# A decoder block with gathered experts: 32 more tokens leave the dense u pass, low parts of u move to GpSimd beside the gates, and v weights are made in pairs

## The chip, the cores and the metric
The kernel runs on one core of one Trainium2 chip. The metric is device time in microseconds, the median of several runs. Engines: TensorE (PE) multiplies matrices, VectorE (DVE), ScalarE (ACT) and GpSimd (POOL) work on elements, SyncE (SP) issues transfers. SBUF is on-chip memory of 128 partitions, PSUM takes TensorE's results.

## The reference
512 tokens of width 1024 pass one block: a norm with modulation, three kinds of attention, an output projection, then a feed-forward part with 16,384 experts, and a last norm. Nearly all the time behind the attention is the expert part:

```python
q = einsum('td,de->te', xc, wq)                  # 8 heads x 2 sides x 128
s = einsum('thpd,hpnd->thpn', q, sub_keys)       # 128 keys a side
sv, si = top_k(s, 16)                            # best keys of each side
cand = sv[:, :, 0, :, None] + sv[:, :, 1, None, :]
top, pos = top_k(cand, 16)                       # 16 experts a head, 128 a token
g = softmax(top)
a = gelu(einsum('thkd,td->thk', u[eidx], x))     # u, v: 16384 x 1024, float32
return einsum('thk,thkd->td', g * a, v[eidx])
```

## The kernel before, in words
The expert part is done in two ways. Tile 0 (128 tokens) is done by gathering: for each of its 128 expert slots GpSimd gathers 128 rows of u and of v, VectorE takes a dot with u and adds v times its weight. The other 384 tokens (DT) are done densely: the experts stand in 128 chunks of 128, and for each chunk TensorE makes all dots of u with all tokens (`a_chunk`, 24 matmuls), the result goes through gelu, is multiplied by a gate that is zero where a token did not choose the expert, and multiplies v (`v_chunk`, 18 matmuls of 512 columns). Float32 is kept by splitting each operand into a rounded high part and a low rest: three products in place of one. ScalarE rounds (`u_hi`, `v_hi`), VectorE or GpSimd subtracts (`u_lo`, `v_lo`).

The order is written out by hand. First the q and score matmuls; VectorE picks the top 16 of each (`best16`, two heads at a time, after every fourth q pass) and decodes numbers (`decode`). Meanwhile TensorE starts on the u chunks. 64 chunks (and chunk 64) come "early": chunks 0 to 23 alone, then for each of three tiles four gate blocks of 32 tokens, with two u chunks beside each block, and gaps of u chunks alone between them (4, 8 and 4 chunks), in which VectorE decodes the next tile. A block has eight groups of four tokens. For a group VectorE makes `hot_i` (four operations: key numbers compared with a token's column, times the gate, L2057) and `hot_j` (L2059); TensorE multiplies them into a table of gates, ScalarE copies it to `g_out` and stores the whole block to DRAM at its end (2 MB). hot_i and hot_j have two buffers. VectorE makes the low part of every u chunk from 17 on (L2002, `split_u`), GpSimd of those before.

Then comes the mixed loop: for each chunk m, v of chunk m, then u of chunk m + 65, as long as there are u chunks (63 times); VectorE multiplies gelu by gate, rounds it and subtracts (`weigh`), makes v's and u's low parts, and works 12 to 14 gathered rows of tile 0 in eight chunks. The last 60 chunks have v alone, less four at the end in another order. Gates come back from DRAM four chunks at a time into g_in (512-byte pieces). The mixed loop can start when the last block's gates are stored and the first group is loaded.

## Time and profile before
| | |
|---|---|
| median of 3 runs | 1567.66 us (1567.62 to 1569.81) |
| span of the profiled execution | 1565.4 us |
| TensorE busy | 1527.4 us (98%) |
| VectorE busy | 1337.7 us (85%) |
| ScalarE busy | 660.1 us (42%) |
| GpSimd busy | 487.5 us (31%) |
| DMA | 398.77 MB, mean 255 GB/s |

The span is from the first to the last instruction of the profiled execution; the profile gives no other time for that execution, and the median of the runs lies 2.3 us above it. Matmuls are pipelined and their ends are modelled, so a busy TensorE can still be slower than it could be; starts say more than durations.

### The profile page before, as it was taken

How to read it: one execution, taken by the hardware profiler on the slowest of the kernel's cores; microseconds unless marked ns; L12 is line 12 of the kernel's file. 1: busy time of each engine (PE TensorE's matmuls, PEld its weight loads, DVE VectorE, ACT ScalarE, POOL GpSimd, SP SyncE). 2: the span in 40 equal slices, each digit the busy share in tenths (PEclk: the TensorE clock that was granted, in tenths of full speed). 3: DMA queues.
4: the chain of work that ended last, by engine and by line, in shares of the span. 5: the costliest groups of instructions: out<-in, count | busy, mean ns of one | idle time of the engine just before them, and what ended most of it. 6: DMA issues, size and time to landing. Idle time of an engine off the chain costs nothing.

```text
span 1565.4 us, 24588 instructions
## 1 busy us (share of the span) xinstructions
PE 1527.4 (98%) x8275; PEld 1363.9 (87%) x8275; DVE 1337.7 (85%) x2877; ACT 660.1 (42%) x1143; POOL 487.5 (31%) x450
## 2 busy tenths in 40 slices
PE   4999999999999999999999999999999999999997
PEld 4887767888999999999999999999999998888886
DVE  5788666549999989899698898899999998999977
ACT  3444554233344757657433333343333332333232
POOL 1121300033450000020355455456566663233000
PEclk9999999999999999999999999999999999999999
DMA  9754410132355565676899999999999999999772
GB/s 366 270 174 148 148 68 0 55 95 82 118 169 180 194 230 199 229 248 251 298 393 330 350 340 343 346 337 371 372 378 372 368 345 355 376 350 352 241 244 104
DMA packets 160467, 398.77 MB, mean 255 GB/s; under 512 B 11753, under 2 KB 75369, under 8 KB 158705
## 3 DMA queue, kind: packets, MB, share of 16 engines
q1 hardware_dynamic: 112992, 227.06, 41.7%
q0 software_dynamic: 36864, 134.23, 23.2%
q10 hardware_dynamic: 10514, 36.30, 5.9%
q8 instruction: 47, 0.77, 0.2%
q14 instruction: 50, 0.41, 0.1%
HBM read 359.27 MB, written 38.27 MB: 254 GB/s over the span
## 4 chain that ended last, share of the span: by engine, by line
PE 83%; DVE 13%; DMA 1%; ACT 1%; issue 1%; ACTq 0%; DVEq 0%; SPq 0%
PE bank_S L907 16%; PE bank_T L907 11%; PE bank_O L858 6%; PE bank_O L856 6%; PE bank_O L857 6%; PE bank_T L885 5%; PE bank_G L907 5%; PE bank_S L856 3%; PE bank_S L857 3%; PE bank_S L858 3%; PE bank_O L643 2%; PE bank_S L610 2%; DVE mod_acc L1909 1%; DVE v_sb L1902 1%; DVE v_sb L1915 1%; DVE si L1921 1%
## 5 line engine op out<-in xcount | busy, mean ns | idle before, releaser
L1462 ACT ACTIVATE v_hi<-v_raw 128x1024 fp32r<-128x1024 f32 x124 | 131.7, 1062 | 333.9 <-PE bank_G L907 330.9
L1434 ACT ACTIVATE u_hi<-u_raw 128x1024 fp32r<-128x1024 f32 x128 | 135.9, 1061 | 243.0 <-PE bank_O L858 122.8
L1213 POOL COPY stage<-eidx 128x1 uint32<-128x1 uint32 (+1 forms) x128 | 75.7, 591 | 461.8 <-DVE eidx L2030 207.7
L1217 POOL DMA_INDIRECT row<-in_peer_u,stage x128 | 148.1, 1157 | 103.8 <-POOL stage L1213 103.8
L856 PE MATMUL bank_S<-h_hi,u_hi 128*128 128x384 f32 x512 | 179.7, 351 | 0.5 <-DVE u_lo L2002 0.5
L858 PE MATMUL bank_O<-h_hi,u_lo 128*128 128x384 f32 x512 | 171.9, 336 | 0.0
L856 PE MATMUL bank_O<-h_hi,u_hi 128*128 128x384 f32 x512 | 171.7, 335 | 0.0
L858 PE MATMUL bank_S<-h_hi,u_lo 128*128 128x384 f32 x512 | 171.5, 335 | 0.0
L857 PE MATMUL bank_O<-h_lo,u_hi 128*128 128x384 f32 x512 | 171.5, 335 | 0.0
L857 PE MATMUL bank_S<-h_lo,u_hi 128*128 128x384 f32 x512 | 171.4, 335 | 0.0
L2098 DVE SCALAR_TENSOR_TENSOR y<-row,wgt,y 128x1024 f32<-128x1024 f32 x128 | 165.9, 1296 | 0.0
L2108 DVE TENSOR_TENSOR v_lo<-v_raw,v_hi 128x1024 fp32r<-128x1024 f32 x124 | 152.0, 1226 | 12.1 <-ACT v_hi L1462 0.6
L2121 DVE SCALAR_TENSOR_TENSOR junk<-row,h 128x1024 f32<-128x1024 f32 x128 | 155.8, 1217 | 0.0
L1217 POOL DMA_INDIRECT row<-in_peer_v,stage x128 | 141.6, 1106 | 41.9 <-issue 30.3
L907 PE MATMUL bank_S<-v_hi,w_lo 128*128 128x512 f32 x372 | 125.4, 391 | 0.0
L907 PE MATMUL bank_S<-v_lo,w_hi 128*128 128x512 f32 x372 | 125.3, 391 | 0.0
L907 PE MATMUL bank_S<-v_hi,w_hi 128*128 128x512 f32 x372 | 125.2, 391 | 0.0
L1505 ACT ACTIVATE g_out<-bank_T 128x512 f32<-128x512 f32 x96 | 104.7, 1122 | 46.6 <-PE bank_T L885 38.2
L2057 DVE TENSOR_SCALAR hot_i<-iota_k,cols 128x128 f32<-128x128 f32 x384 | 106.6, 341 | 1.0 <-PE bank_T L885 0.2
L885 PE MATMUL bank_T<-hot_i,hot_j 128*128 128x128 f32 x768 | 101.8, 275 | 1.2 <-DVE hot_j L2059 1.2
L885 PEld LDWEIGHTS bank_T<-hot_i,hot_j 128*128 128x128 f32 x768 | 97.6, 191 | 3.6 <-issue 2.1
L856 PEld LDWEIGHTS bank_O<-h_hi,u_hi 128*128 128x128 f32 x512 | 96.1, 188 | 2.5
(370 smaller groups left out, 3647.8 us busy)
## 6 DMA issues: line engine op xcount, KB each, us to landing
u_raw<-in_u_t SPq DMA_DIRECT2D x128, 512.0 KB
v_raw<-in_peer_v SPq DMA_DIRECT2D x128, 512.0 KB
gates<-g_out ACTq DMA_DIRECT2D x12, 2048.0 KB, 6.8
g_in<-gates SPq DMA_DIRECT2D x32, 768.0 KB
ada_late<-in_w_ada SPq DMA_DIRECT2D x8, 2048.0 KB, 8.4
spill<-a_act ACTq DMA_DIRECT2D x56, 192.0 KB, 2.1
a_act<-spill SPq DMA_DIRECT2D x14, 768.0 KB, 10.6
w_raw<-in_w_in SPq DMA_DIRECT2D x20, 512.0 KB, 4.1
```

The costliest lines, as they stand in the source:

```text
L856: pe.matmul(ps[:, 0:DT], u_hi[q][:, kk], h_hi[:, GT:NT, k, :], start=(k == 0), stop=False)
L857: pe.matmul(ps[:, 0:DT], u_hi[q][:, kk], h_lo[:, GT:NT, k, :], start=False, stop=False)
L858: mm = pe.matmul(ps[:, 0:DT], u_lo[q][:, kk], h_hi[:, GT:NT, k, :], start=False, stop=(k == KD - 1))
L885: mm = pe.matmul(ps[:, tok * P:tok * P + P], hot_j[:, b % 2, tok, :], hot_i[:, b % 2, tok, :], start=True, stop=True)
L907: mm = pe.matmul(y_bank[t][half][:, :], w[:, q, tt], v[:, q, half * 512:half * 512 + 512], start=(first and n == 0), stop=False)
L1217: pool.indirect_dma_start(rows[slot][:, :], None, table[:, :], bass.IndirectOffsetOnAxis(stage[:, place:place + 1], 0))\
L1434: act.activation(u_hi[c % 2][:, :], u_raw[:, c % 2, :], ACT.Copy).then_inc(s_uhi, 1)
L1462: act.activation(v_hi_end[:, i % TAIL, :] if end else v_hi[:, c % 2, :], v_raw[c % 4][:, :], ACT.Copy)\
L2057: dve.tensor_scalar(hot_i[:, B % 2, tok, :], iota_k[:, :], cols[:, 0, n:n + 1], cols[:, 2, n:n + 1], ALU.is_equal, ALU.mult)
L2098: dve.scalar_tensor_tensor(out=y0[:, :], in0=rows[2 * place + 1][:, :], scalar=wgt[:, q], in1=y0[:, :], op0=ALU.mult, op1=ALU.add).then_in ...
L2108: dve.tensor_tensor(lo[:, q, :], v_raw[c % 4][:, :], hi[:, q, :].bitcast(f32), ALU.subtract)\
L2121: dve.scalar_tensor_tensor(out=junk[:, :], in0=rows[2 * place][:, :], scalar=1.0, in1=h2[:, 0, :], op0=ALU.mult, op1=ALU.mult, accum_out=d ...
```

## The change
- 32 more tokens (x: the last quarter of tile 3) leave the dense u pass: its matmuls have 352 columns. Their dots are made from gathered u rows, 32 gathers of 128 rows (32 tokens by 4 quarters of the slots), with h2 of these tokens copied to all four quarters (`h2x`). GpSimd gathers into 5 places, VectorE makes the 32 dots between its other early work (DOTS_AFTER, DOTS_BESIDE). Gelu and gate of x are multiplied before the gates are made (`gates_of_x`), so the gates of x hold the whole weight; v stays as it was.
- The blocks are done in another order: 8, 9, 10 (tile 3), 0 to 3, 4 to 7, and last the block of x. Gaps: 24, 5, 5, 3 and 3 chunks.
- Low parts of u beside gates, and of the chunk behind each run of blocks, are made by GpSimd. hot_j reads its key numbers from PSUM; hot_i reads them from SBUF as before.
- The first four q passes' scores are taken in two halves, so that the first head is chosen after two passes.
- Gates are stored by group of four chunks (g_in comes back as 6 KB a partition). SyncE stores a block's gates, but the last block of a run is stored by ScalarE in quarters, over the chunks of the gap that follows.
- v weights come in pairs of chunks: one product in place in g_in (VectorE), one rounding copy (ScalarE, `w_high`), one subtraction (VectorE, `w_low`), each of twice the elements.

```diff
+XT = 32
+DX = DT - XT
+XN = 32
+X_BLOCK = BLOCKS - 1
+QUARTERS = P // XT
+X_PLACES = 5
+PHASES = [[8, 9, 10], [0, 1, 2, 3], [4, 5, 6, 7], [X_BLOCK]]
+PHASE_TILE = [3, 1, 2, 3]
+GAPS = [24, 5, 5, 3]
+def early_plan():
+    between, beside, i = [], {}, 0
+    for gap, blocks in zip(GAPS, PHASES):
+        between.append(range(i, i + gap))
+        i += gap
+        for tb in blocks:
+            beside[tb] = i
+            i += 2
+    between.append(range(i, EARLY))
+    return between, beside
+BETWEEN, BESIDE = early_plan()
+PLACE_OF = {tb: o for o, tb in enumerate(tb for blocks in PHASES for tb in blocks)}
+FIRST_LOW = 17
+LOW_ON_POOL = set(range(FIRST_LOW)) | {i for p, blocks in enumerate(PHASES)
+                                       for i in range(BESIDE[blocks[0]], BETWEEN[p + 1].start + 1)}
+DOTS_AFTER = {23: 4, 31: 2, 32: 2, 33: 2, 34: 2, 44: 2, 45: 2, 46: 2, 47: 3}
+DOTS_BESIDE = 1
...
-        g_in = at("g_in", 56, [P, 2, DT // GB, 4, GB])
+        a_act = at("a_act", 20, [P, AHEAD, DX])
+        y0 = at("y0", 32, [P, KD, S])[:, :, 0:P]
+        g_in = [at(f"g_in{j}", kib, [P, DT // GB, 4, GB]) for j, kib in enumerate((56, 182))]
...
-        u_lo = [at(f"u_lo{j}", kib, [P, D], f32r) for j, kib in enumerate((92, 84))]
+        u_lo = [at("u_lo0", 92, [P, KD, P], f32r)[:, :, :], h_lo[:, :, 0:P]]
...
+        rows_x = [at(f"row_x{j}", k, [P, D]) for j, k in enumerate((108, 136, 168, 84, 104))]
...
-        gates = nc.dram_tensor("gates", [DT // GB, P, NCHUNK, GB], f32).ap()
-        spill = nc.dram_tensor("spill", [SPILL, P, DT], f32).ap()
+        gates = nc.dram_tensor("gates", [P, NCHUNK // 4, DT // GB, 4, GB], f32).ap()
+        spill = nc.dram_tensor("spill", [SPILL // 4, P, 4, DX], f32).ap()
...
-                    pe.matmul(ps[:, 0:DT], u_hi[q][:, kk], h_hi[:, GT:NT, k, :], start=(k == 0), stop=False)
...
+                    pe.matmul(ps[:, 0:DX], u_hi[q][:, kk], h_hi[:, k, GT * P:S - XT], start=(k == 0), stop=False)
...
+            def last_and_columns(phase):
+
+                last = BETWEEN[phase][-1]
                 a_chunk(last, last, range(KD // 2))
-                ps = take("G", ("cols", tile))
-                pe.wait_ge(s_idx, tile + 1)
-                for n, m in enumerate((key_f[:, tile + GT, 0, :], key_f[:, tile + GT, 1, :], gate[:, tile + GT, :])):
-                    mm = pe.transpose(ps[:, n * P:n * P + P], m, ident[:, :])
+                tile = PHASE_TILE[phase]
+                ps = take("G", ("cols", phase))
+                if PHASES[phase] == [X_BLOCK]:
+                    pe.wait_ge(s_xgate, 1)
+                    mm = pe.transpose(ps[:, 0:P], gate[:, tile, :], ident[:, :])
+                else:
+                    pe.wait_ge(s_idx, phase + 1)
+                    for n, m in enumerate((key_f[:, tile, 0, :], key_f[:, tile, 1, :], gate[:, tile, :])):
+                        mm = pe.transpose(ps[:, n * P:n * P + P], m, ident[:, :])
                 mm.then_inc(full["G"], 1)
                 a_chunk(last, last, range(KD // 2, KD))
...
+            sp.wait_ge(s_h2, NT)
+            for q in range(QUARTERS):
+                sp.dma_start(h2x[q * XT:q * XT + XT, :], h2[P - XT:P, H2_SLOT[NT - 1], :]).then_inc(s_hx, 16)
...
+            def store_gates(tb):
+                o = PLACE_OF[tb]
+                sp.wait_ge(s_gt, (o + 1) * (GB // 4))
+                sp.dma_start(gates[:, :, tb, :, :].rearrange("p q i t -> p q (i t)"),
+                             g_out[o % 2][:, :, :].rearrange("p (q i) t -> p q (i t)", i=4)).then_inc(s_gst[o % 2], 16)
+            STORES = {BESIDE[tb] + 4: tb for tb in BESIDE if not last_of_phase(tb)}
             for i in range(2, EARLY):
                 load_u(i, i)
+                if i in STORES:
+                    store_gates(STORES[i])
...
+                if i > 0 and i - 1 not in LOW_ON_POOL:
+                    pool.wait_ge(s_ulo, i)
                 pool.wait_ge(s_uhi, i + 1)
-                pool.tensor_tensor(u_lo[c % 2][:, :], u_raw[:, c % 2, :], u_hi[c % 2][:, :].bitcast(f32),
+                pool.tensor_tensor(u_lo[c % 2], by_k(u_raw[:, c % 2, :]), by_k(u_hi[c % 2][:, :]).bitcast(f32),
                                    ALU.subtract).then_inc(s_ulo, 1)
...
+            def gather_x(first, end):
+                for n in range(first, min(end, XN)):
+                    place = n % X_PLACES
+                    if n >= X_PLACES:
+                        pool.wait_ge(s_xdot, n + 1 - X_PLACES)
+                    pool.indirect_dma_start(rows_x[place][:, :], None, peer_u[:, :],
+                                            bass.IndirectOffsetOnAxis(eidx_x[:, n:n + 1], 0)).then_inc(s_got_x[place], 16)
+            pool.wait_ge(s_xidx, QUARTERS)
+            got = X_PLACES
+            gather_x(0, got)
+            for phase, blocks in enumerate(PHASES):
+                for i in range(BESIDE[blocks[0]], BETWEEN[phase + 1].start + 1):
+                    ready = dots_before(i) + X_PLACES
+                    gather_x(got, ready)
+                    got = max(got, ready)
+                    split_u(i, i)
+                ready = dots_before(BETWEEN[phase + 1].stop) + X_PLACES
+                gather_x(got, ready)
+                got = max(got, ready)
+            pool.wait_ge(s_xdot, XN)
...
+            def w_high(i, c):
+                if not within(i):
+                    return
+                if at_end(i):
+                    act.wait_ge(s_acc, PH * TOPK)
+                else:
+                    after(act, s_yv, i - 2)
+                act.wait_ge(s_pw, over(i, c, 2) + 1)
+                act.activation(weight_pair(w_hi, w_hi_end, i, c), gate_pair(c), ACT.Copy).then_inc(s_whi, 1)
...
+            def store_quarter(tb, h):
+                o = PLACE_OF[tb]
+                if h == 0:
+                    act.wait_ge(s_gt, (o + 1) * (GB // 4))
+                act.dma_start(gates[:, 8 * h:8 * h + 8, tb, :, :].rearrange("p q i t -> p q (i t)"),
+                              g_out[o % 2][:, 32 * h:32 * h + 32, :].rearrange("p (q i) t -> p q (i t)", i=4))\
+                   .then_inc(s_gst[o % 2], 16)
+            def gelu_of_x():
+                act.wait_ge(s_xdot, XN)
+                for q in range(QUARTERS):
+                    act.activation(gelu_x[P - XT:P, q * XN:q * XN + XN], dots_x[q * XT:q * XT + XT, :], ACT.Gelu)\
+                       .then_inc(s_xgelu, 1)
...
+                stored, gap = 0, BETWEEN[phase + 1]
+                for n, i in enumerate(gap):
                     u_high(i + 2, i + 2)
                     early_gelu(i)
+                    while stored < 4 and (stored + 1) * len(gap) <= 4 * (n + 1):
+                        store_quarter(blocks[-1], stored)
+                        stored += 1
+                    if phase == len(PHASES) - 2 and n == 0:
+                        gelu_of_x()
...
+            act.wait_ge(s_gst[1], 16 * stores_of(BLOCKS - 1))
+            w_high(0, 0)
...
                     gelu(m + EARLY, c, c)
+                if c % 2 == 0:
+                    w_high(m + 2, c + 2)
...
+            for i in range(NT):
+                emptied(dve, ("sc_first", i))
+                choose(0, i, 0, 1)
+            for i in range(NT):
+                emptied(dve, ("sc", 0, i))
+                choose(0, i, 1, 1)
+            for g in range(1, 4):
+                for i in range(NT):
+                    emptied(dve, ("sc", g, i))
+                    choose(g, i, 2 * g, 2)
...
-                if i == FIRST_LOW:
-                    dve.wait_ge(s_ulo, i)
-                if i >= FIRST_LOW:
+                if i not in LOW_ON_POOL:
+                    if i - 1 in LOW_ON_POOL:
+                        dve.wait_ge(s_ulo, i)
                     dve.wait_ge(s_uhi, i + 1)
-                    dve.tensor_tensor(u_lo[i % 2][:, :], u_raw[:, i % 2, :], u_hi[i % 2][:, :].bitcast(f32),
+                    dve.tensor_tensor(u_lo[i % 2], by_k(u_raw[:, i % 2, :]), by_k(u_hi[i % 2][:, :]).bitcast(f32),
                                       ALU.subtract).then_inc(s_ulo, 1)
...
+            def index_x():
+                for q in range(QUARTERS):
+                    part, slots = slice(q * XT, q * XT + XT), slice(q * XN, q * XN + XN)
+                    dve.scalar_tensor_tensor(out=eidx_x[part, :], in0=key_f[P - XT:P, NT - 1, 0, slots],
+                                             scalar=float(NKEYS), in1=key_f[P - XT:P, NT - 1, 1, slots],
+                                             op0=ALU.mult, op1=ALU.add).then_inc(s_xidx, 1)
+            dotted = [0]
+            def x_dot():
+                n = dotted[0]
+                dotted[0] += 1
+                row = rows_x[n % X_PLACES]
+                dve.wait_ge(s_got_x[n % X_PLACES], 16 * (n // X_PLACES + 1))
+                dve.scalar_tensor_tensor(out=row[:, :], in0=row[:, :], scalar=1.0, in1=h2x[:, :],
+                                         op0=ALU.mult, op1=ALU.mult, accum_out=dots_x[:, n:n + 1]).then_inc(s_xdot, 1)
+            def split_and_dot(n):
+                split_u(n)
+                for _ in range(DOTS_AFTER.get(n, 0)):
+                    x_dot()
+            def gates_of_x():
+                own = gate[P - XT:P, NT - 1, :]
+                dve.wait_ge(s_xgelu, QUARTERS)
+                dve.tensor_tensor(own, own, gelu_x[P - XT:P, :], ALU.mult).then_inc(s_xgate, 1)
...
+            iota_p = bank[turn[("q", 2 * PH - 2)][0]][:, 0:NKEYS]
+            dve.tensor_copy(iota_p, iota_k[:, :]).then_inc(s_iota, 1)
+            dve.wait_ge(s_iota, 1)
+            dve.wait_ge(s_hx, 16 * QUARTERS)
...
+                if phase == 0:
+                    first = FIRST_LOW + 3
+                    decode(NT - 1, s_dv, [([first], [], [first + 1]), ([], [first + 2], [])])
                     normalise()
-                    rest = list(range(first + 3, last))
+                    index_x()
...
+                    decode(0 if phase == len(PHASES) - 1 else phase, s_idx,
+                           [([], rest[0:1], rest[1:2]), ([], rest[2:3], rest[3:4])])
                     rest = rest[4:]
-                if tile == NT - GT - 1:
-                    decode(0, s_idx, [([], rest[0:1], rest[1:2]), ([], rest[2:3], rest[3:4])])
...
+                if PHASES[phase] == [X_BLOCK]:
+                    gates_of_x()
+                    ps = taken(dve, ("cols", phase))
+                    dve.tensor_copy(cols[:, 2, DX:DT], ps[:, P - XT:P]).then_inc(freeing(("cols", phase)), 1)
...
+                    for b in range(GB // 4):
+                        B = PLACE_OF[tb] * (GB // 4) + b
+                        after(dve, s_gm, B - 1)
+                        for tok in range(4):
+                            n = GB * tb + 4 * b + tok
+                            dve.tensor_scalar(hot_i[:, B % 2, tok, :], iota_k[:, :], cols[:, 0, n:n + 1],
+                                              cols[:, 2, n:n + 1], ALU.is_equal, ALU.mult)
+                        n = GB * tb + 4 * b
+                        dve.tensor_tensor(hot_j[:, B % 2, :, :], iota_p.unsqueeze(1).to_broadcast([P, 4, P]),
+                                          cols[:, 1, n:n + 4].unsqueeze(2).to_broadcast([P, 4, P]),
+                                          ALU.is_equal).then_inc(s_hot, 1)
+                        if b == 5 and tb != X_BLOCK:
+                            for _ in range(DOTS_BESIDE):
+                                x_dot()
...
-            def weigh(i, c, late):
-                dve.wait_ge(s_g[(c // 4) % 2], 16 * (over(i, c, 8) + 1))
+            def product(i, c):
+                if not within(i):
+                    return
+                late = isinstance(i, int) and i >= MAIN
+                dve.wait_ge(s_g[c // 4 % 2], 16 * (over(i, c, 8) + 1))
                 if late:
-                    dve.wait_ge(s_al[c // 4], 2 * (i - c) - 2 * MAIN + 16)
+                    dve.wait_ge(s_al[c // 4 % 2], 16 * ((i - MAIN) // AHEAD + 1))
                 else:
-                    dve.wait_ge(s_gelu, i + SPILL + 1)
-                dve.tensor_tensor(w_f[:, :].rearrange("p (b t) -> p b t", t=GB),
-                                  a_act[:, c, :].rearrange("p (b t) -> p b t", t=GB),
-                                  g_in[:, (c // 4) % 2, :, c % 4, :], ALU.mult).then_inc(s_pw, 1)
-                dve.wait_ge(s_pw, i + 1)
-                end = at_end(i)
-                hi, lo = (w_hi_end, w_lo_end) if end else (w_hi, w_lo)
-                q = i % TAIL if end else c % 2
-                if not end:
-                    after(dve, s_yv, i - 1)
-                dve.tensor_copy(hi[:, q, :], w_f[:, :]).then_inc(s_whi, 1)
-                dve.wait_ge(s_whi, i + 1)
-                dve.tensor_tensor(lo[:, q, :], w_f[:, :], hi[:, q, :].bitcast(f32), ALU.subtract)\
-                   .then_inc(s_w, 1)
-                dve.wait_ge(s_w, i + 1)
+                    dve.wait_ge(s_gelu, i + SPILL + 2)
+                slot = c % AHEAD
+                own = gate_pair(c)[:, :, 0:DX // GB, :]
+                dve.tensor_tensor(own, by_block(a_act[:, slot:slot + 2, :]), own, ALU.mult)\
+                   .then_inc(s_pw, 1)
+            def w_low(i, c):
+                dve.wait_ge(s_whi, over(i, c, 2) + 1)
+                if not at_end(i):
+                    after(dve, s_yv, i - 2)
+                dve.tensor_tensor(weight_pair(w_lo, w_lo_end, i, c), gate_pair(c),
+                                  weight_pair(w_hi, w_hi_end, i, c).bitcast(f32), ALU.subtract).then_inc(s_w, 1)
...
-                weigh(i, c, late)
+                if c % 2 == 0:
+                    w_low(i, c)
+                else:
+                    product(i + 1, c + 1)
```

## Rows read from the trace of the kernel before

**Rows 1.** The page, the chain of work that ended last, by engine
```profile
PE 83%; DVE 13%; DMA 1%; ACT 1%; issue 1%; ACTq 0%; DVEq 0%; SPq 0%
```

**Rows 2.** Busy us of each engine (x instructions), clock, DMA share, GB/s by stage
```profile
406.30:508.50 102.20, 101.37 (x584) 100.28 (x583) 96.61 (x456) 46.29 (x60) 38.37 (x16) 1.00 0.53 168
508.50:570.50 62.00, 61.93 (x446) 61.29 (x447) 61.56 (x165) 44.88 (x48) 0.00 (x0) 1.00 0.51 189
570.50:588.50 18.00, 17.62 (x103) 17.27 (x102) 13.99 (x22) 6.90 (x10) 0.00 (x0) 1.00 0.81 291
650.50:684.90 34.40, 34.05 (x198) 33.69 (x196) 27.16 (x39) 12.38 (x18) 3.14 (x4) 1.00 0.69 236
746.90:768.00 21.10, 21.10 (x124) 21.10 (x123) 9.49 (x10) 9.58 (x13) 1.47 (x3) 1.00 0.78 274
768.00:1291.40 523.40, 523.40 (x2648) 476.58 (x2647) 484.79 (x631) 197.04 (x396) 304.21 (x312) 1.00 0.97 358
1291.40:1540.30 248.90, 248.90 (x1099) 206.13 (x1099) 220.52 (x322) 79.01 (x116) 48.75 (x62) 1.00 0.89 312
```

**Rows 3.** Timeline of TensorE (start, us), 256 columns; then chain, mixed loop
```profile
65.72 0.28 PE L583 MATMUL bank_G<-w_in_hi,h_lo 128*128 128x256 f32 x1
...
70.04 0.28 PE L583 MATMUL bank_S<-w_in_hi,h_lo 128*128 128x256 f32 x1
...
1158.47 1.62 PE bank_S L907 x7
1166.78 1.62 PE bank_S L907 x7
```

**Rows 4.** Timelines of VectorE and of GpSimd, beside the gates
```profile
684.70 1.11 DVE L2057 TENSOR_SCALAR hot_i<-iota_k,cols 128x128 f32<-128x128 f32 x4
...
686.33 1.11 DVE L2057 TENSOR_SCALAR hot_i<-iota_k,cols 128x128 f32<-128x128 f32 x4
...
684.75 0.33 POOL L1213 COPY stage<-eidx 128x1 uint32<-128x1 uint32 x1
...
688.87 2.07 POOL L1213 COPY stage<-eidx 128x1 uint32<-128x1 uint32 x1
```

**Rows 5.** VectorE by line, operation and shape: busy us, mean ns
```profile
L2057 DVE TENSOR_SCALAR hot_i<-iota_k,cols 128x128 f32<-128x128 f32 x384 | 106.6, 341 | 1.0 <-PE bank_T L885 0.2
L2059 DVE TENSOR_TENSOR hot_j<-iota_k,cols 128x512 f32<-128x512 f32 x96 | 65.6, 683 | 0.0
L2002 DVE TENSOR_TENSOR u_lo<-u_raw,u_hi 128x1024 fp32r<-128x1024 f32 x48 | 58.6, 1221 | 23.9 <-ACT u_hi L1434 23.5
...
L1669 DVE TENSOR_SCALAR h<-bank_S,a_col,m_cols 128x512 f32<-128x512 f32 x2 | 1.6, 804 | 0.0
...
L1971 DVE TENSOR_SCALAR v_sb<-v_sb 128x512 f32<-128x512 f32 x1 | 0.4, 427 | 0.0
```

**Rows 6.** Timeline of VectorE, the first choice of the top 16
```profile
337.25 0.88 DVE L1902 MAX8 v_sb<-sc 128x8 f32<-128x128 f32 x4 [21.76 <-ACT sc L1426]
```

**Rows 7.** Timelines of VectorE and GpSimd in the score stage
```profile
342.46 0.50 DVE L1939 TENSOR_TENSOR mod_acc<-v_sb 128x32 f32<-128x32 f32 x4
...
350.41 1.83 DVE L1939 TENSOR_TENSOR mod_acc<-v_sb 128x32 f32<-128x32 f32 x4
...
349.50 2.39 POOL L1186 TENSOR_TENSOR wq_lo<-wq_raw,wq_hi 128x1024 fp32r<-128x1024 f32 x1 [3.96 <-ACT wq_hi L1367]
```

**Rows 8.** DMA issues by line (us to landing); timelines of SyncE and GpSimd
```profile
gates<-g_out ACTq DMA_DIRECT2D x12, 2048.0 KB, 6.8
...
759.40 0.38 SPq L1092 DMA_DIRECT2D g_in<-gates  x1
...
765.42 0.18 POOL L1213 COPY stage<-eidx 128x1 uint32<-128x1 uint32 x1 [70.47 <-DMA g_in<-gates]
```

**Rows 9.** Busy us and DMA of the mixed loop, early
```profile
783.00:822.00 39.00, 39.00 (x197) 35.28 (x196) 37.75 (x51) 13.76 (x26) 22.81 (x24) 1.00 1.02 392
```

292 lines of the change are left out of this document (163 added, 129 removed).

## The prediction

> **What bounds the kernel now.** I read the chain of waits first: TensorE holds most of it and VectorE nearly all the rest [rows 1]. Then the busy time by stage [rows 2], cut where the work changes: u chunks alone (406.3 to 508.5 us), three runs of four gate blocks, the gaps between them, the mixed loop (768.0 to 1291.4) and the v loop. TensorE is full in all of them. A matmul record lasts longer than its share of the array, so the reader should look at starts: in the v loop 1,099 matmuls of 512 columns take 248.9 us, 0.2265 each, and a chunk of 18 takes 4.08 us [rows 2]. In the mixed loop one chunk follows another after 8.31 us [rows 3]; less 4.08, its 24 u matmuls of 384 columns take 4.23, or 0.176 each. Both loops are TensorE's. The granted clock is 1.00 (the 2.4 GHz level) in every stage to 1540 us [rows 2].
>
> Beside the gates there is a second bound: VectorE is busy 61.56 of 62.0 us [rows 2]. One group of four tokens costs it 1.63 us (686.33 less 684.70) [rows 4]; eight groups are 13.1, two u splits of about 1.15 (1.22 long, overlapping a little [rows 5]) bring a block to 15.4, and TensorE needs 15.5 (62.0 by four). Two engines are balanced to 1%. What the change does to that balance decides this case.
>
> **1. Narrower u matmuls.** 352 columns in place of 384. Matmuls of 256 columns start every 0.12 us (36 steps in 4.32 us [rows 3]), those of 512 every 0.2265: 0.42 ns a column, so 32 columns save 13.3 ns a matmul and 0.32 us a chunk of 24. The mixed loop runs 63 such chunks with TensorE full: **-20.2 us**. The other end is 0, if something else takes the loop over. In the early stage 65 chunks are worth 20.8 more, if VectorE lets TensorE have it.
>
> **2. Pairs of v weights.** A pair costs VectorE one product and one subtraction; the rounding copy goes to ScalarE, and each instruction's fixed part is paid once in two chunks. VectorE's load in the mixed loop (484.79 of 523.4 us [rows 2]) falls; ScalarE has 326 us idle there. TensorE sets both loops, so 0, and this keeps VectorE from being the bound at 7.99 us a chunk. The v loop is unchanged: 0. If the new path through ScalarE cost each pair a wait of 0.5 us, 62 pairs would be 31 us; I take 0, since the product is made a whole chunk ahead.
>
> **3. Earlier top-16.** VectorE stood idle 21.76 us before its first choice at 337.25 [rows 6]. The new order starts it after two q passes fewer, 10.9 us of matmuls (48 at 0.2265) and their score matmuls: about 12.7. The first eight choices are half size and pay their fixed parts twice, some 5 us in all, so about 7 us are left when VectorE comes to decode. TensorE wants its 24 chunks 7.7 us earlier. So far a draw.
>
> **4. The first dots.** Then VectorE must index (about 1 us), wait for the first gathered row, and do four dots, each as long as a split, 1.2 us [rows 5] before it copies the columns and makes the first hot rows (2.3 us). From indices to four dots done I take 11: 1.1 to issue, 3.5 for 512 KB (between the 1.3 that they take at 392 GB/s [rows 9] and the 6.0 of g_in's 768 KB [rows 8]), then four rows at 1.2 to 1.7 us. Chunk 23 ends near 501, the first gates start near 509; before they started at 508.5. **+0.5**, that is, the whole 7.7 of the first 24 chunks is lost. Bounds: -6 with the rows there at once, +4 with slow gathers.
>
> **5. Low u on GpSimd beside the gates.** The two splits of a block leave VectorE (-2.3) and one dot comes (+1.2): 14.3 us, under TensorE's new 14.86 (15.5 less 0.64). That would be right if nothing collided. But a GpSimd split takes 2.39 us, and one of its low parts can be seen against a VectorE operation [rows 7]: four small adds that take 0.50 us take 1.83 when GpSimd started at 349.50; they begin to move when it ends at 351.89. A two-input VectorE operation stands still for as long as GpSimd has the port. The change shields hot_j from this by reading the numbers from PSUM. Does hot_i suffer? It has one tensor input. Its time tells how it reads: 512 elements with two per-partition scalars, from PSUM, take 804 ns; at 1.05 ns an element (683 for 512, 1,221 for 1,024), 128 elements would take 401; hot_i takes 341 [rows 5]. It is fast, as the 427 ns of a one-input operation of 512 within SBUF is. And GpSimd feels it: a copy that takes 0.18 us alone [rows 8] took 0.33, ending 0.13 after the first of four hot_i (684.70, 0.256 each), and another took 2.07 through hot_i, hot_j and a split [rows 4]. So hot_i uses what GpSimd needs, and I take the lock to work both ways. A split then enters between two hot_i (2.39 us lost) or at a hot_j, which runs beside it (1.8 lost). I take 2.0: a block is 14.3 + 4.0 = 18.3 us. Eleven such blocks and a last one without dot (17.2) are 218.5 us, before 12 x 15.5 = 186: **+32.5**. Bounds: 178 us if hot_i doesn't wait (-8), 229 at 2.4 a split (+43).
>
> The Trainium skill (SBUF — State Buffer, "Who interferes with whom") says that a VectorE instruction in a two-port mode, tensor_scalar among them, and a GpSimd instruction exclude each other for the whole instruction, whichever came first. The trace has no hot_i behind a GpSimd split, so no row shows that half. By the rule the block is the 18.3 of above; by the rows of two-input operations alone, which leave hot_i free, it is 14.9.
>
> **6. The gaps.** They were 18.0, 34.4 and, with chunk 64, 21.1 us [rows 2]. The new first gap has five chunks, 19.3 us of TensorE. VectorE was busy 13.99 us in the old one; eight dots and the decode step that no longer fits ahead make it 25, plus 1.5 waiting for the first high u; TensorE is 2 us behind VectorE at its start, so it lasts 24.4. The second has nine dots: 25.6. The third (three chunks, tile 0's decode, the gates of x) has 13 to 15 us of VectorE against 11.6: 13.2. VectorE runs out of lead since in part 5 it has none.
>
> The last gap: gates used to be stored whole at the end of their block, four chunks before they were needed. Now the last two quarters are issued by ScalarE after the gelu of chunk 63, with one chunk left to hide them. 2 MB landed in 6.8 us, and g_in came 6.0 us after its issue (759.40 to 765.42) [rows 8]. I take 5.5 for 1 MB in short pieces, 4 for g_in in long ones, 0.4 to issue, and 3 for product, high and low: 13 us from 1.5 after chunk 63, of which chunk 64 covers 3.9. So 15.4 + 10 = 25.4. Bounds of this wait: 6 and 13.
> Gaps together 88.6 for 73.5: **+15.1**.
>
> **7. What else moves.** SyncE's new gate stores wait for a block's last g_out with the u loads behind them; beside gates a chunk takes 8 us or more and a u tile is loaded two chunks ahead, so 0. If a store of 512-byte pieces delays a load in the same queue, it is by up to 5 us, still inside those two chunks. GpSimd's gathers wait for a dot with the low u of the next chunk behind them; dot and gather come in the middle of a block, some 8 us before that chunk: 0. The stores of quarters on ScalarE stand behind a gelu that has passed: 0 except for the last, above. The other layouts (h by column, y0 strided, gates by group of four chunks) keep each instruction's elements: 0.
>
> **Sum.** +0.5 + 32.5 + 15.1 - 20.2 = +27.9 on the span of 1565.4, so 1593.3; the median lies 2.3 above that span, so **1595 us**.
>
> **Rivals.**
> - *hot_i is free of GpSimd.* Then blocks are 14.86 and VectorE keeps its lead; gaps are 85.7: +0.5 - 8 + 12.2 - 20.2 = -15.5, **1552 us, faster**. For it: no row shows hot_i waiting. Against: [rows 4, 5]. The sign turns where a block takes 16.1 us, a loss of 0.9 us per split.
> - *GpSimd collides but the waits of parts 4 and 6 are half as long* (rows and gates land quickly, u is there): 11 to 18 us less, **1580 us**. The times of [rows 8] were taken beside other loads, which speaks for it.
> - *Transfers bound the mixed loop.* Its chunks of two parts and 1.75 rows move 3.08 MB; at 7.99 us that is 385 GB/s. The loop has moved 392 for 39 us [rows 9], so I expect it to fit; at 371 (the same 3.08 MB in 8.31 us, all that before shows for long) 31 of them would lose 0.31 us each: **1605 us**. Against it also: g_in now comes in 6 KB pieces.
>
> **How the numbers follow.** Chances: forecast 0.45, half waits 0.17, transfers 0.08, hot_i free 0.30. The forecast's own range is 1583 to 1608: 17.8 to 19.1 a block, 6 to 13 for the last wait. The range must hold the free case's upper part: 1550 to 1608. About 0.2% is what a measurement can tell here. Faster 0.31, within 0.2% 0.04, slower 0.65.
>
> **What would show it.** Mixed loop: v matmuls of successive chunks 7.99 us apart, v loop 4.08. Gate blocks: groups of four hot_i that take some 3 us where a GpSimd u_lo runs, 1.1 elsewhere; TensorE waiting for hot_j. First gates near 509 and 5 to 8 us of TensorE idle before them; some 10 us idle before the first v matmul, behind the stores of the last quarters. I am wrong if hot_i takes 1.1 beside GpSimd, if the last quarters land during chunk 64, or if the pairs' path makes TensorE wait in the loops.

## The result, and the profile after

The changed kernel takes 1647.35 us (median; 1641.45 to 1649.75), the kernel before 1567.64 in the same series: a ratio of 1.050, 95% interval 1.048 to 1.052. It is 80 us slower. I had forecast 1595 and a range to 1608: the side was right, the size was not. The profiled execution, the longest of the four, has a span of 1648.0 us, against 1593.3 in my sum.

The page of the changed kernel, the chain by engine, and two groups of instructions (busy us, mean ns, idle before):

```profile
PE 70%; DVE 25%; DMA 2%; ACT 1%; issue 1%; POOL 0%; ACTq 0%; SPq 0%; DVEq 0%
...
L2299 DVE TENSOR_SCALAR hot_i<-iota_k,cols 128x128 f32<-128x128 f32 x384 | 166.2, 495 | 23.9 <-PE bank_T L984 22.5
...
L984 PE MATMUL bank_T<-hot_i,hot_j 128*128 128x128 f32 x768 | 118.2, 304 | 60.2 <-DVE hot_j L2302 57.6
```

VectorE's share of the chain has gone from 13 to 25% [rows 1]. The same 384 hot_i cost 166.2 us in place of 106.6 [rows 5], 59.6 more; VectorE stood 22.5 us ahead of them, waiting for TensorE (0.2 before [rows 5]); and TensorE waited 57.6 us for hot_j (1.2 before), 9.5 of it at the first gates. The stages of the changed kernel, by the windows view (columns as in [rows 2]), are cut at TensorE's first gates and then where VectorE starts and ends a run of blocks:

```profile
408.40:520.90 112.50, 96.64 (x583) 93.67 (x581) 101.55 (x474) 46.44 (x60) 49.22 (x26) 0.96 0.54 178
520.90:583.10 62.20, 50.06 (x314) 48.03 (x315) 57.96 (x122) 29.75 (x32) 19.05 (x10) 0.86 0.58 181
583.10:609.50 26.40, 24.21 (x140) 23.65 (x140) 22.93 (x35) 9.13 (x12) 9.56 (x7) 0.91 0.72 251
609.50:695.60 86.10, 67.53 (x434) 65.02 (x434) 79.46 (x168) 42.20 (x46) 26.08 (x14) 0.89 0.65 202
695.60:722.70 27.10, 24.91 (x144) 24.34 (x143) 23.99 (x36) 9.12 (x12) 10.07 (x8) 0.91 0.73 252
722.70:806.10 83.40, 67.20 (x436) 64.69 (x435) 76.60 (x169) 42.65 (x47) 24.27 (x10) 0.90 0.58 183
806.10:822.80 16.70, 12.90 (x85) 12.64 (x84) 13.72 (x19) 6.98 (x12) 2.67 (x1) 1.00 0.36 106
822.80:844.20 21.40, 17.47 (x105) 16.65 (x105) 15.27 (x40) 9.26 (x11) 6.47 (x5) 0.84 0.72 246
844.20:871.50 27.30, 17.84 (x115) 17.58 (x113) 7.98 (x9) 10.11 (x13) 6.75 (x10) 0.87 0.86 286
871.50:1374.50 503.00, 503.00 (x2650) 458.22 (x2651) 448.61 (x503) 219.13 (x429) 320.11 (x312) 1.00 0.97 372
1374.50:1623.00 248.50, 248.50 (x1098) 205.78 (x1097) 188.42 (x201) 101.06 (x146) 72.20 (x62) 1.00 0.83 308
```

From the start of the u chunks to the first v matmul it was 361.7 us (406.3 to 768.0); now it is 463.1. The table sets these rows against the forecast; its five differences add up to the 54.7 us by which the span exceeds my sum.

| | forecast | measured | off by |
|---|---|---|---|
| start of the u chunks | 406.3 | 408.4 | +2.1 |
| u chunks to the first gates | 102.7 | 112.5 | +9.8 |
| gate blocks (62.2 + 86.1 + 83.4 + 21.4) | 218.5 | 253.1 | +34.6 |
| gaps (26.4 + 27.1 + 16.7 + 27.3) | 88.6 | 97.5 | +8.9 |
| first v matmul to the end | 777.2 | 776.5 | -0.7 |

**One gate block.** Timelines of VectorE, GpSimd and TensorE in the changed kernel, from one dot to the next (start, us):

```profile
556.58 3.78 DVE L2299 TENSOR_SCALAR hot_i<-iota_k,cols 128x128 f32<-128x128 f32 x4
...
563.20 1.12 DVE L2299 TENSOR_SCALAR hot_i<-iota_k,cols 128x128 f32<-128x128 f32 x4 [0.61 <-PE bank_T L984]
...
565.54 1.12 DVE L2299 TENSOR_SCALAR hot_i<-iota_k,cols 128x128 f32<-128x128 f32 x4 [0.63 <-PE bank_T L984]
...
567.40 3.22 DVE L2299 TENSOR_SCALAR hot_i<-iota_k,cols 128x128 f32<-128x128 f32 x4
...
577.16 3.79 DVE L2299 TENSOR_SCALAR hot_i<-iota_k,cols 128x128 f32<-128x128 f32 x4
```
```profile
557.91 2.36 POOL L1320 TENSOR_TENSOR u_lo<-u_raw,u_hi 128x1024 fp32r<-128x1024 f32 x1
...
567.64 2.38 POOL L1320 TENSOR_TENSOR h_lo<-u_raw,u_hi 128x1024 fp32r<-128x1024 f32 x1 [7.37 <-ACT u_hi L1581]
```
```profile
556.43 1.05 PE L984 MATMUL bank_T<-hot_i,hot_j 128*128 128x128 f32 x8
561.11 2.05 PE L984 MATMUL bank_T<-hot_i,hot_j 128*128 128x128 f32 x8 [2.67 <-DVE hot_j L2302]
...
571.37 1.13 PE L984 MATMUL bank_T<-hot_i,hot_j 128*128 128x128 f32 x8 [1.19 <-DVE hot_j L2302]
```

(`h_lo` in GpSimd's second row is the second buffer of u_lo.) Two groups of four hot_i hold a GpSimd subtraction and take 3.78 and 3.22 us; the others take 1.1. The block lasts 577.16 - 556.58 = 20.58 us: 8 x 1.63 + 1.14 for the dot + 2.67 + 2.11 lost, and 1.2 for VectorE's two waits for TensorE (the rest, 0.4, is in shorter ones). Such waits come to 0.2 us in the whole kernel before. Their source is in the gate matmuls, 2.05 us in place of 1.05, and in the granted clock, by the windows view of these microseconds:

```profile
556.70:559.00 2.30, 1.74 (x13) 1.45 (x12) 2.30 (x4) 1.93 (x2) 2.04 (x2) 1.00 0.49 171
559.00:561.00 2.00, 0.00 (x0) 0.00 (x0) 2.00 (x3) 0.00 (x0) 1.27 (x1) 0.92 0.65 223
561.00:563.00 2.00, 1.89 (x9) 1.92 (x10) 1.59 (x5) 0.00 (x0) 0.00 (x0) 0.50 0.74 229
563.00:565.00 2.00, 2.00 (x12) 2.00 (x12) 1.72 (x5) 1.09 (x1) 0.00 (x0) 0.73 0.08 33
565.00:567.00 2.00, 2.00 (x18) 2.00 (x17) 1.46 (x5) 1.46 (x2) 0.00 (x0) 1.00 0.00 0
```

TensorE has no record at all from 559 to 561, waiting for hot_j; when it starts again the granted clock is 0.50 (the 1.2 GHz level, half of 2.4) and is back at 1.00 by 565. So this collision is paid twice: VectorE stands still, then TensorE is slow, and VectorE, two buffers ahead at most, waits for it. The second collision of the block, with no dot in front of it, makes TensorE wait 1.19 us, and its eight matmuls take 1.13: it is paid once.

**First gates.** VectorE's timeline of the changed kernel: the index, and the first dot.

```profile
504.69 0.84 DVE L2236 SCALAR_TENSOR_TENSOR eidx_x<-v_sb 32x32 uint32<-32x32 f32 x4
...
513.49 1.23 DVE L2248 SCALAR_TENSOR_TENSOR row_x<-row_x,h2x 128x1024 f32<-128x1024 f32 x1 [6.70 <-DMA row_x<-in_peer_u,eidx_x]
```

**Last gaps.** The chain of the changed kernel, and one line each of SyncE's and ScalarE's timelines from the gap before:

```profile
852.87 6.08 DMA u_raw<-in_u_t
859.55 4.69 DMA gates<-g_out
864.31 4.00 DMA g_in<-gates
868.39 0.91 DVE g_in L2325
```
```profile
822.72 0.43 SPq L1180 DMA_DIRECT2D u_raw<-in_u_t  x1
```
```profile
828.54 1.06 ACT L1581 ACTIVATE u_hi<-u_raw 128x1024 fp32r<-128x1024 f32 x1 [10.79 <-DMA u_raw<-in_u_t]
```

The u tile issued at 822.72 stood in SyncE's queue behind a v load that waits until the columns of the block of x are taken, and ScalarE waited 10.79 us for it, with its g_out copies behind.

### The profile page after: what moved, and what is told of

It reads as the page before. It is cut to its first block, busy times and chain, and to the rows that moved or that the text cites. A ratio compares the mean times of both kernels' runs of the same rounds, so it can differ in the third digit from the quotient of the medians.

```text
span 1648.0 us, 24337 instructions
## 1 busy us (share of the span) xinstructions
PE 1529.2 (93%) x8276; PEld 1358.2 (82%) x8276; DVE 1346.7 (82%) x2680; ACT 700.2 (42%) x1215; POOL 630.3 (38%) x510
## 4 chain that ended last, share of the span: by engine, by line
PE 70%; DVE 25%; DMA 2%; ACT 1%; issue 1%; POOL 0%; ACTq 0%; SPq 0%; DVEq 0%
PE bank_S L1006 15%; PE bank_T L1006 10%; DVE hot_i L2299 7%; PE bank_G L1006 5%; PE bank_O L947 5%; PE bank_O L949 5%; PE bank_O L948 5%; PE bank_T L984 3%; DVE hot_j L2302 2%; DVE row_x L2248 2%; PE bank_O L729 2%; PE bank_S L696 2%; DVE mod_acc L2123 2%; DVE mod_acc L2093 1%; DVE v_sb L2099 1%
## 5 line engine op out<-in xcount | busy, mean ns | idle before, releaser
L1337 POOL DMA_INDIRECT row<-in_peer_v,stage x128 | 185.6, 1450 | 42.3 <-issue 38.3
L947 PE MATMUL bank_S<-h_hi,u_hi 128*128 128x352 f32 x512 | 183.6, 359 | 10.9 <-DVE h_lo L2201 5.1
L2299 DVE TENSOR_SCALAR hot_i<-iota_k,cols 128x128 f32<-128x128 f32 x384 | 166.2, 495 | 23.9 <-PE bank_T L984 22.5
L984 PE MATMUL bank_T<-hot_i,hot_j 128*128 128x128 f32 x768 | 118.2, 304 | 60.2 <-DVE hot_j L2302 57.6
L948 PE MATMUL bank_S<-h_lo,u_hi 128*128 128x352 f32 x512 | 172.2, 336 | 0.0
L947 PE MATMUL bank_O<-h_hi,u_hi 128*128 128x352 f32 x512 | 165.9, 324 | 0.0
L948 PE MATMUL bank_O<-h_lo,u_hi 128*128 128x352 f32 x512 | 164.9, 322 | 0.0
L1685 ACT ACTIVATE g_out<-bank_T 128x512 f32<-128x512 f32 x96 | 102.7, 1108 | 129.8 <-PE bank_T L984 121.7
L2369 DVE SCALAR_TENSOR_TENSOR row<-row,h 128x1024 f32<-128x1024 f32 x128 | 156.1, 1220 | 0.0
L947 PEld LDWEIGHTS bank_S<-h_hi,u_hi 128*128 128x128 f32 x512 | 103.3, 202 | 14.9 <-issue 12.3
L948 PEld LDWEIGHTS bank_S<-h_lo,u_hi 128*128 128x128 f32 x512 | 103.1, 201 | 0.0
L948 PEld LDWEIGHTS bank_O<-h_lo,u_hi 128*128 128x128 f32 x512 | 96.9, 189 | 2.5
## 6 DMA issues: line engine op xcount, KB each, us to landing
g_in<-gates SPq DMA_DIRECT2D x32, 768.0 KB, 8.0
```

Source lines behind the costliest of these rows:

```text
L947: pe.matmul(ps[:, 0:DX], u_hi[q][:, kk], h_hi[:, k, GT * P:S - XT], start=(k == 0), stop=False)
L948: pe.matmul(ps[:, 0:DX], u_hi[q][:, kk], h_lo[:, k, GT * P:S - XT], start=False, stop=False)
L984: mm = pe.matmul(ps[:, tok * P:tok * P + P], hot_j[:, b % 2, tok, :], hot_i[:, b % 2, tok, :], start=True, stop=True)
L1337: pool.indirect_dma_start(rows[slot][:, :], None, table[:, :], bass.IndirectOffsetOnAxis(stage[:, place:place + 1], 0))\
L1685: act.activation(g_out[o % 2][:, :, 4 * b:4 * b + 4].rearrange("p i t -> p t i"), bank[f"T{b % 2}"][:, :].rearrange("p (t i) -> p t i", t= ...
L2299: dve.tensor_scalar(hot_i[:, B % 2, tok, :], iota_k[:, :], cols[:, 0, n:n + 1], cols[:, 2, n:n + 1], ALU.is_equal, ALU.mult)
```

## The experiments

Each kernel is the changed one with the edit shown, unless it says otherwise. Ratios are to the kernel before, with 95% intervals; times are medians of four. In the diffs `...` stands for what is not shown.

**Is it GpSimd?** Three edits on the same suspect: taken off GpSimd, hot_i taken off SBUF, and GpSimd's work made short.

```diff
-LOW_ON_POOL = set(range(FIRST_LOW)) | {i for p, blocks in ...}
+LOW_ON_POOL = set(range(FIRST_LOW))
...
-                    split_u(i, i)
...
+                        if b % 4 == 3:
+                            split_u(BESIDE[tb] + b // 4 + 1)
```

> The changed kernel, but VectorE makes the low parts of all u chunks beside the gates again, and GpSimd none behind chunk 16. Theory A (a GpSimd subtraction stops hot_i for its whole length): groups of four hot_i take 1.1 us everywhere, a gate block costs VectorE 8 x 1.63 + 2.3 for two low parts + 1.2 for a dot = 16.5 us in place of 20.2 to 20.6, so about 4 us less in each of 12 blocks, 1600 us (1594 to 1607). Theory B (the blocks are slow because TensorE, after each idle time, runs at a lower granted clock and its gate matmuls of eight take 2.05 us; GpSimd does little): blocks stay above 19 us and the time above 1630.

```diff
-                            dve.tensor_scalar(hot_i[...], iota_k[:, :], cols...
+                            dve.tensor_scalar(hot_i[...], iota_p, cols...
```

> The changed kernel, but hot_i reads its numbers from the copy in PSUM, as hot_j does. Theory A, in the form that only operations on SBUF alone are stopped: no group of four hot_i above 2 us, each a little slower (0.32 to 0.40 us in place of 0.26), a block 8 x 1.7 to 1.9 + 1.2 = 15 to 16.5 us, in all 1600 us (1590 to 1612). If GpSimd stops VectorE whatever it reads, the groups of 3.2 to 3.7 us stay, and the time is 1650 to 1665. Theory B: blocks above 19 us, the time not under 1635.

```diff
+                ks = slice(0, 1) if i >= FIRST_LOW else slice(0, KD)
-                pool.tensor_tensor(u_lo[c % 2], ...
+                pool.tensor_tensor(u_lo[c % 2][:, ks, :], ...
```

> The changed kernel, but each GpSimd subtraction behind chunk 16 covers 128 of its 1024 columns (the rest of the low part is left out), so that it is some eight times shorter and everything else stays. Theory A: the loss follows GpSimd's length; groups of four hot_i take at most 1.6 us, VectorE needs 14.3 + 0.8 a block and TensorE 14.9, so 15.2 us a block, a granted clock of 1.00 beside the gates, and some 1580 us (1573 to 1590). Theory B: the blocks stay above 18 us with a clock of 0.9.

Measured: 1590.2 (1.0142, 1.0125 to 1.0159), 1596.8 (1.0182, 1.0165 to 1.0199) and 1577.6 us (1.0057, 1.004 to 1.0073), so 57, 51 and 70 us less than the changed kernel. All three came out as theory A has it (the first 4 us below its range), and far under the 1630 that theory B asks for. The second run of blocks in each, by the windows view, first VectorE's low parts, then hot_i from PSUM, then the short ones:

```profile
597.70:662.80 65.10, 61.73 (x447) 58.92 (x448) 65.10 (x173) 44.95 (x48) 3.75 (x4) 1.00 0.82 249
```
```profile
595.70:660.00 64.30, 60.61 (x446) 58.53 (x447) 64.26 (x165) 43.64 (x48) 24.18 (x13) 1.00 0.83 255
```
```profile
593.00:655.90 62.90, 61.14 (x453) 59.55 (x451) 60.98 (x170) 43.26 (x48) 9.05 (x14) 1.00 0.87 277
```

Four blocks took 86.1 us; here 65.1, 64.3 and 62.9 by these windows, with the clock at 1.00 again. The windows are not cut quite alike: from VectorE's first hot_i to its last hot_j the four runs last 86.2, 64.7, 64.7 and 61.4 us. In the first two VectorE is busy without a break: it is the bound at 16.1 to 16.3 us a block. And even with GpSimd's work nearly gone, 1577.6 is still 9 above the kernel before in its series. The run with hot_i from PSUM also shows what is still stopped. VectorE's timeline in it, then GpSimd's:

```profile
709.23 1.38 DVE L2299 TENSOR_SCALAR hot_i<-bank_S,cols 128x128 f32<-128x128 f32 x4
...
711.10 3.25 DVE L2248 SCALAR_TENSOR_TENSOR row_x<-row_x,h2x 128x1024 f32<-128x1024 f32 x1
```
```profile
703.38 2.39 POOL L1320 TENSOR_TENSOR h_lo<-u_raw,u_hi 128x1024 fp32r<-128x1024 f32 x1 [4.92 <-ACT u_hi L1581]
710.87 2.40 POOL L1320 TENSOR_TENSOR u_lo<-u_raw,u_hi 128x1024 fp32r<-128x1024 f32 x1 [5.11 <-ACT u_hi L1581]
```

A group of hot_i reading PSUM takes 1.4 us beside GpSimd or not, 0.25 more than one that reads SBUF and meets nothing; a dot with two SBUF inputs, started 0.23 after GpSimd, takes 3.25 in place of 1.22. Two dots are stopped so in this kernel's third run of blocks, which takes 69.7 us where the second takes 64.7. The Trainium skill (SBUF — State Buffer, "Who interferes with whom") says that a VectorE instruction with two SBUF inputs contends with a GpSimd instruction that reads SBUF, that one in a two-port mode contends with GpSimd, and that one with at most one SBUF input outside those modes does not. The runs agree, by these numbers, if hot_i from SBUF is in such a mode, which only its time (341 ns [rows 5]) tells.

**The same part alone, in the kernel before.** GpSimd makes the low parts of its 27 chunks beside the gates, nothing else is changed.

```diff
         FIRST_LOW = 17
+        LOW_ON_POOL = set(range(FIRST_LOW)) | set(range(24, 33)) | set(range(36, 45)) | set(range(52, 61))
...
```

> The kernel before with one part of the change alone: GpSimd makes the low parts of the 27 chunks beside the gates. hot_i and hot_j both read SBUF. Each subtraction then stops VectorE for 2.0 to 2.4 us and saves it 1.15: VectorE 13.1 + 4.0 to 4.8 = 17.1 to 17.9 us a block against 15.4, 12 blocks: 20 to 30 us slower, 1588 to 1598. If the loss in the changed kernel came only together with the dots and late waits, TensorE stays the bound at 15.5 and the time within 5 us of 1568.

1605.3 us (1.0236, 1.0219 to 1.0253), 37 slower and more than expected. A group of its VectorE timeline, with GpSimd's beside it:

```profile
545.81 3.27 DVE L2060 TENSOR_SCALAR hot_i<-iota_k,cols 128x128 f32<-128x128 f32 x4 [0.22 <-PE bank_T L886]
```
```profile
546.62 2.38 POOL L1203 TENSOR_TENSOR u_lo<-u_raw,u_hi 128x1024 fp32r<-128x1024 f32 x1 [7.19 <-ACT u_hi L1437]
```
```profile
508.30:579.80 71.50, 63.56 (x444) 60.93 (x445) 69.90 (x157) 44.41 (x48) 20.51 (x8) 1.00 0.48 176
```

The last line is its first run of blocks: 17.9 us a block, 2.4 more than before, and a granted clock of 1.00. The three runs give 71.5 + 72.2 + 72.1 for 186, the last gap 5 more. So the part alone makes the kernel slower, with no dot, no narrower matmul and no fall of the clock: TensorE's waits for hot_j in these runs are 1.5 us or less. In the changed kernel the waits are 2.0 to 3.8 us at one collision of nearly every block, and the clock falls to 0.50 at or soon after most of them. In the block above it is the collision behind the dot; that the dot makes the difference fits this, but no run moves the dot alone. Nor is the length of the wait the whole of it: in the kernel with low parts on VectorE, TensorE waited 2.74 us at 689.74 and the clock stayed at 1.00.

**The start and the first gates.**

```diff
-DOTS_AFTER = {23: 4, 31: 2, 32: 2, 33: 2, 34: 2, ...}
+DOTS_AFTER = {31: 3, 32: 3, 33: 3, 34: 3, ...}
```

> The changed kernel, but the four dots that stand ahead of the first gates are done in the first gap (three dots behind each of its last four chunks in place of two). If the first gates waited for the gathered rows and these dots, their first matmul comes at 511 in place of 520.9 and 4.6 us come back in the first gap: 1642 us (1639 to 1645). The rival: the first block's own dot then waits for the rows with the gates behind it, and nothing is gained: 1645 to 1650.

```diff
-            for i in range(NT): ... choose(0, i, 0, 1)
-            for i in range(NT): ... choose(0, i, 1, 1)
+            for i in range(NT): ... choose(0, i, 0, 2)
```

> The changed kernel, but the first choice is made for two heads at once again, after four q passes (ScalarE's two copies stay). The half choices cost VectorE some 12 us of fixed parts and of standing behind GpSimd's low parts of wq; so VectorE starts 11 us later and comes to the gates at the same time: experts of x indexed at 505 (503 to 507), and 1647 us (1641 to 1652). If the half choices cost only the 5 us of the forecast, the gates come 6 to 7 us later: 1652 to 1656.

Without the four dots the first gates come at 512.9 in place of 520.9, as expected, but the time, 1644.4 us (1.049, 1.0472 to 1.0507), can't be told from 1647: executions of either kernel differ by 8 us, more than the 3 to 5 that are looked for. What is shown is the wait, not its net worth. With the whole choice it is 1641.9 us (1.0462, 1.0444 to 1.0479), 5 us less, at the edge of what can be told apart. First choice and index in the kernel with whole choices, by VectorE's timeline, then the first choice in the changed kernel:

```profile
338.87 0.87 DVE L2086 MAX8 v_sb<-sc 128x8 f32<-128x128 f32 x4 [21.54 <-ACT sc L1569]
...
502.24 0.83 DVE L2233 SCALAR_TENSOR_TENSOR eidx_x<-v_sb 32x32 uint32<-32x32 f32 x4
```
```profile
326.17 0.49 DVE L2086 MAX8 v_sb<-sc 128x8 f32<-128x128 f32 x2 [8.85 <-ACT sc L1573]
...
329.05 0.43 DVE L2123 TENSOR_TENSOR mod_acc<-v_sb 128x16 f32<-128x16 f32 x4
...
339.25 2.07 DVE L2123 TENSOR_TENSOR mod_acc<-v_sb 128x16 f32<-128x16 f32 x4
```
```profile
338.63 2.40 POOL L1302 TENSOR_TENSOR wq_lo<-wq_raw,wq_hi 128x1024 fp32r<-128x1024 f32 x1 [3.95 <-ACT wq_hi L1509]
```

Starting 12.7 us later, VectorE indexes 2.4 us earlier (502.24 against 504.69): 163.4 us from choice to index against 178.5. The index comes between 502.5 and 506.2 in the kernels with half choices, so the 2.4 are within what executions differ by, but the 12.7 us of head start are gone. Most of them went to one kind of instruction: the small adds of the top-16 (L2123) take 24.7 us ahead of the index with half choices and 13.3 without. With halves, six of the first eight groups of four adds take 2.06 us in place of 0.43, as the last lines show for one: each lies beside one of GpSimd's low parts of wq, which come every 6.35 us, and a held half choice takes just as long.

**Dots, columns, stores.**

```diff
-                dve.scalar_tensor_tensor(out=row[:, :], in0=row[:, :], ..., in1=h2x[:, :],
+                dve.scalar_tensor_tensor(out=row[:, 0:128], in0=row[:, 0:128], ..., in1=h2x[:, 0:128],
```

> The kernel with low parts of u on VectorE (1590.2), but each of the 32 dots of x covers 128 of 1024 columns (the rest is left out), some 1.0 us less each. If VectorE's own time bounds the early stage, up to 32 us come back, less where TensorE takes over (a block 15.4 in place of 16.3, the gaps of 26 us shorter by 8): 1564 us (1560 to 1571), about the kernel before. The rival: the rows' transfers and other waits bound the gaps, and the first gates wait for the gathered rows (6 us) whatever the dots cost: 1575 to 1582.

1578.5 us (1.0069, 1.0052 to 1.0086): 12 us less than 1590.2, not the 26 that VectorE's time would allow; the rival was right. Its first gates come at 520.0 against 521.6, hardly earlier, as the four dots still start 1.24 us apart, each waiting for its row; TensorE waited 9.8 us there.

```diff
-                    pe.matmul(ps[:, 0:DX], u_hi[q][:, kk], h_hi[:, k, GT * P:S - XT], ...
+                    pe.matmul(ps[:, 0:DT], u_hi[q][:, kk], h_hi[:, k, GT * P:S], ...
```

> The changed kernel with u matmuls of 384 columns again (the 32 additional results are not used). Mixed loop: 63 chunks x 0.32 = 20 us longer (503 to 523). In the early stage nothing if VectorE and the waits set it: 1667 us (1663 to 1672). The rival: TensorE's lower granted clock makes its time count beside the gates too, 0.32 us or more for each of 65 chunks: 1680 or more.

1670.4 us (1.0652, 1.0634 to 1.067). Its mixed loop lasts 523.4 us against 503.0, so the narrower matmuls are worth 20.4 there. The medians differ by 23.1; the 2.7 left for the early stage are within what executions differ by.

```diff
-                    while stored < 4 and (stored + 1) * len(gap) <= 4 * (n + 1):
+                    while stored < 4 and (phase == len(PHASES) - 1 or (stored + 1) * len(gap) <= 4 * (n + 1)):
...
-                m = i - (EARLY - 5)
+                m = i - (EARLY - 4)
```

> The changed kernel with two orders altered: the four quarters of the last block's gates are stored behind the first chunk of the last gap, all together, in place of behind its first, second and third; and SyncE's loads of the first v rows, which wait for the gates of x, stand one u chunk later in its queue. If these two waits set the ends of the last two gaps, the u tile that was issued at 822.7 and waited 11 us comes earlier (3 to 7 us) and the last store lands 4 to 7 us earlier: 1637 us (1633 to 1642). The rival: VectorE and the loads of u set both gaps anyway, and four stores at once slow those loads: 1644 to 1650.

1642.2 us (1.0482, 1.046 to 1.0504), not told apart from the changed kernel. The block of x lasts 18.8 us by VectorE's timeline in place of 21.6, but in the three kernels before this one (later dots, whole choice, wide matmuls), where the u tile still waits 10 us, it lasts 18.4, 17.5 and 18.6: that the edit shortens it is not shown. The last gap did not get shorter (28.2 against 27.3), and ScalarE's timeline shows what stood in it:

```profile
840.39 1.28 ACTq L1667 DMA_DIRECT2D gates<-g_out  x2
841.26 0.45 ACT L1632 ACTIVATE a_act<-bank_S 128x352 f32<-128x352 f32 x1
841.69 8.16 ACTq L1667 DMA_DIRECT2D gates<-g_out  x2
850.23 1.06 ACT L1581 ACTIVATE u_hi<-u_raw 128x1024 fp32r<-128x1024 f32 x1 [8.53 <-issue]
```

Two stores are issued in 1.28 us, the next two in 8.16, and the rounding copy behind them comes 8.5 us late.

**Can the rest be had back?** Combinations of these edits. The third to fifth store the last gates at the block's end; the last three let hot_i read PSUM only in the groups that GpSimd should meet.

> Three edits together: low parts of u on VectorE beside the gates, the four first dots in the first gap, stores and v loads as in the third edit. If their effects add (1590 measured for the first, 3 to 5 for the second, 5 to 10 for the third): 1578 us (1573 to 1584), still slower than the kernel before by some 9. If VectorE bounds the whole early stage and the other waits only lay beside it: 1585 to 1590.

> hot_i reads PSUM, the dot beside the gates stands behind the third group in place of the sixth, away from GpSimd's subtraction (in the run with PSUM alone two dots of four took 3.25 us there in place of 1.22), and the first dots and the stores are moved as above. Blocks 8 x 1.87 + 1.14 = 16.1 us each, no dot of 3 us; 1597 less 5 for the dots, 4 for the first gates, 5 to 8 for the stores: 1580 us (1574 to 1586). If GpSimd stops something else in its place, 1590 or more.

> The three edits together (1581.3), with the four quarters of the last gates stored right at the end of their block, ahead of the next rounding copy. The stores are issued some 8 us earlier (776 in place of 784.4) and take about 8 us to land: the first v matmul comes 4 to 8 us earlier, 1575 us (1572 to 1578). The rival: the stores then run beside the u and v loads, which come late in their place, and nothing is gained: 1580 to 1583.

```diff
-                            dve.tensor_scalar(hot_i[...], iota_k[:, :], cols...
+                            dve.tensor_scalar(hot_i[...], iota_p if b in (2, 3, 5, 6) else iota_k[:, :], cols...
```

> Low parts of u on GpSimd as in the changed kernel, but hot_i reads PSUM in four of eight groups of a block, those (2, 3, 5, 6) beside which GpSimd subtracts, and the dot stands behind group 4; first dots and last stores as in the run before. VectorE: 8 x 1.63 + 4 x 0.25 + 1.14 = 15.2 us a block against TensorE's 14.9, in place of 16.3: 11 blocks x 1.1 = 12 us less than 1575, so 1563 us (1560 to 1570), faster than the kernel before. If GpSimd's starts move by a group, some groups are stopped for 2 us and the time is 1575 to 1590.

> The same with six groups (1, 2, 3, 5, 6, 7) from PSUM: 15.7 us a block, but room for GpSimd's starts to move: 1569 us (1566 to 1574). If four groups are enough it is 5 to 6 us slower than that run; if their starts move, it is the faster one.

> As the run with six groups from PSUM (1585.1), but the last gates are stored behind the first chunk of the last gap, since the stores at the block's end held ScalarE's queue. The last gap becomes 25.5 us in place of 30.5: 1580 us (1577 to 1583). If the longer gap came from GpSimd, 1584 to 1587.

| | us | ratio (95%) |
|---|---|---|
| low parts on VectorE, dots and stores moved | 1581.3 | 1.0080 (1.0063 to 1.0096) |
| hot_i from PSUM, dots and stores moved | 1585.3 | 1.0106 (1.0089 to 1.0123) |
| low parts on VectorE, stores at the block's end | 1580.2 | 1.0079 (1.0063 to 1.0096) |
| PSUM in four groups of eight | 1591.3 | 1.0148 (1.0131 to 1.0165) |
| PSUM in six groups | 1585.1 | 1.0111 (1.0094 to 1.0128) |
| the same, stores one chunk later | 1584.7 | 1.0102 (1.0085 to 1.0119) |

None is faster than the kernel before. The first is 9 us under the 1590.2 of its own first edit: moving the first dots and the stores, which showed nothing in the changed kernel, is worth that here, the two together (its first gates come at 511.7 in place of 521.6). Storing at the block's end gains nothing on it, as the rival had it: the four stores hold ScalarE's queue for 7.2 us.

With four groups the time is 28 us above what I expected. GpSimd's starts move, but only in the first groups of a run: four groups of hot_i that read SBUF are stopped there, for 6.20 and 5.47 us (two subtractions in each), 3.63 and 2.75. That is some 14 us; the stores hold ScalarE's queue for 11.5 us, and the last gap takes 31 us. With six groups, expected at 1569, the second run's four blocks take 63.5 us, 15.9 each, near the 15.7 worked out, and the third's 66.3. In its last gap the stores hold ScalarE's queue for 11.3 us, the rounding copy behind them is late, and TensorE waits 10.3 us for the low part of that chunk. In the last run, where I had expected the later place to help, they hold it for 10.0 us and the last gap is 30 us again, in the rival's range. The queue is not all of it: with hot_i from PSUM alone, where the stores are spread over the chunks, the last gap is 30.2 us too; it is 27.3 in the changed kernel, and 26 to 27 where VectorE makes the low parts. What GpSimd's subtractions do to that gap stays open.

## Why the prediction was wrong in size

- **Narrower matmuls (-20.2)**: right. 503.0 us for 63 chunks, 7.98 each (forecast 7.99), and 20.4 by the run with wide ones. The early stage gave nothing that can be seen: VectorE and the waits set it.
- **Pairs of v weights (0)**: the v loop is 248.5 against 248.9, and TensorE is full in both loops.
- **Earlier top-16 (7 us left)**: wrong. The half choices cost not some 5 but 15.1 us of VectorE, by the run without them; 11.4 of them are the small adds. They pay fixed parts twice, which I had counted, and they fall into step with GpSimd's low parts of wq, which I had not, though [rows 7] shows one such stop: the collision of part 5 at another place. (No run takes GpSimd away there.)
- **First dots (+0.5)**: 9.8 off. Index to four dots done took 13.7 us (504.69 to 518.41), not 11: from the first gather's issue to the first dot it was 7.7 us, where I had 4.6. And the 7 us of lead were not there.
- **Low u on GpSimd (+32.5)**: the step that failed most; the blocks grew by 67.1 us, from 186 to 253.1. Its kind was right: hot_i is stopped, as [rows 4, 5] let me infer, and the rival in which it is free is refuted by every group of 3 us and by three runs. Two things in it were wrong. The collisions were sized at 24 times 2.0 us, 48 in all; there are 28, as GpSimd also makes one more low part in each run of blocks, and the 59.6 us by which hot_i grew are 2.13 for each, 11.6 more than I had. And VectorE's waits for TensorE in the blocks were put at nothing without a reason; they are 22.5 us. Together these make 34.1 of the 34.6 us. In the block shown the waits follow the fall of the clock to 0.50, and in the kernel before with this part alone, where the clock stays at 1.00, they are 5.1 us in all. Some 6 of the 22.5 are in the last block, where TensorE stood 2.55 us for ScalarE's g_out, itself behind the late u tile. That wait in SyncE's queue, behind a v load, is in no part of my sum: part 7 costed only gate stores there, at nothing.
- **Gaps (+15.1)**: they grew by 24.0. The first two 1.5 to 2.0 too short, the third 3.5, the last 1.9. The last wait went as written: store 4.69, g_in 4.00, then product, high and low.
- **Small slips**: the upper bound of the blocks is 228 and not 229, and 1593.3 with 2.3 is 1595.6. Neither changes the forecast.
- **Rivals**: transfers did not bound the mixed loop (372 GB/s, 7.98 us a chunk). Half waits are refuted for the first gates, where the row took longer and not shorter; the last store and g_in took about what I had.
- **Where the 80 us are**: 57 go by the medians when VectorE makes the low parts again (60.6 between the two profiled executions, 1648.0 and 1587.4), 55.8 of them in the blocks (50.9 + 65.1 + 65.3 + 16.0 = 197.3 in place of 253.1; cut alike they differ by 1 to 4 us more). The other 23 are seen in that run against the kernel before: first gates 13.1 later (521.6 against 508.5), blocks 11.3 longer (197.3 against 186), gaps 18.6 longer (92.1 against 73.5), less 20.2 in the loop. What of this is the dots' own time and what their waits is settled only in part: short dots gave 12.
- The 2.1 us that the changed kernel is late before its u chunks arise in the attention stage and were not traced.

## What to carry to other kernels

Where two engines are balanced to 1%, price a move of work by what the receiver does to the giver while it runs, not by the work that leaves: here 1.15 us left VectorE and 2.1 to 2.7 came back. Count every instruction of a moved step at the edges of its loops too, look for every other place where two-input work now falls beside GpSimd, and ask of each stall whether the engine behind it may come back at the lower clock. If VectorE must share with GpSimd, let the exposed instruction read PSUM: hot_i paid 0.06 us each for it and the kernel won back 51 us, though not enough to pay here.

## What was not expected of the hardware

- Four stores of 512 KB in 512-byte pieces, one behind another, held ScalarE's queue for 8.2 to 11.5 us in five kernels, and for 4.1 and 7.2 in the two that make the low parts of u on VectorE. Spread over chunks each took 0.4 to 0.5 us to issue (0.9 in one kernel).
- Gathers of 128 rows by GpSimd start 1.24 us apart behind the first (508.13, 509.38, 510.62), and the first row was used 7.7 us after its issue began (505.83 to 513.49).
